# Expert layer: second-key picks from dot 176, four groups a dot; VectorE makes the first keys' one-hots of all tokens; loads asked for when a place comes free

## What is computed

```python
q = (xn @ wq).reshape(B, L, 8, 256)
s1, s2 = q[..., :128] @ k1, q[..., 128:] @ k2      # scores of first and second keys
v1, i1 = top_k(s1, 16); v2, i2 = top_k(s2, 16)
top_s, pos = top_k(v1[..., :, None] + v2[..., None, :], 16)
idx = i1 * 128 + i2 at pos                          # expert = first key, second key
h = gelu(U[idx] . x)                                # 128 dots a token
w = softmax(top_s) * h
y = sum over the 128 experts of w * V[idx]
```

## Time and profile before

| | us |
|---|---|
| median of 3 runs | 3921.55 (3917.01 to 3927.07) |
| profiled execution, its own time | 3927.68 |
| its span in the trace | 3926.0 |
| TensorE busy | 3713.0 (95%) |
| VectorE busy | 1619.5 (41%) |
| GpSimd busy | 876.8 (22%) |
| ScalarE busy | 662.3 (17%) |
| TensorE's granted clock, mean | 0.977 of full |

### The profile page before, as it was taken

One profiled execution on the slowest core, in us unless ns is written; L12 is line 12 of the kernel. 1 busy time (PEld: TensorE's weight loads), 2 busy tenths in 40 slices (PEclk: granted clock), 3 DMA queues, 4 the chain that ended last, 5 costly groups with the idle time before them and its releaser, 6 DMA issues. The chain is left out here.

```text
span 3926.0 us, 43545 instructions
## 1 busy us (share of the span) xinstructions
PE 3713.0 (95%) x17442; PEld 3168.7 (81%) x17442; DVE 1619.5 (41%) x3495; ACT 662.3 (17%) x1544; POOL 876.8 (22%) x781
## 2 busy tenths in 40 slices
PE   8999999999999999992787999998999999999999
PEld 6878887888888888882676777776888899999888
DVE  5883011100000798656546544445234544444200
ACT  0002102100011122220386100000221122222100
POOL 0001000000000344447743455554100111112000
PEclk9999989999999999996999999999999999999999
DMA  5434432344554799998774699998333322222342
GB/s 213 141 129 149 139 108 81 134 150 150 195 198 167 258 375 381 390 384 286 239 230 146 252 337 331 342 333 318 125 118 125 122 92 92 88 85 68 139 155 100
DMA packets 158692, 771.97 MB, mean 197 GB/s; under 512 B 19444, under 2 KB 21388, under 8 KB 122780
## 3 DMA queue, kind: packets, MB, share of 16 engines
q1 hardware_dynamic: 100248, 514.33, 37.1%
q0 software_dynamic: 57344, 251.69, 17.8%
q10 hardware_dynamic: 900, 3.17, 0.2%
HBM read 760.57 MB, written 8.54 MB: 196 GB/s over the span
## 5 line engine op out<-in xcount | busy, mean ns | idle before, releaser
L355 PE MATMUL PS<-mem,ring 128*128 128x256 f32 (+1 forms) x4608 | 1035.8, 388 | 3.0 <-DMA ring<-in_first_tiles 3.0
L355 PEld LDWEIGHTS PS<-mem,ring 128*128 128x128 f32 x4608 | 883.3, 192 | 154.1 <-issue 5.3
L1995 PE MATMUL PS<-mem,ring 128*128 128x256 f32 x2816 | 640.1, 383 | 9.9 <-DVE ring L2393 9.9
L1995 PEld LDWEIGHTS PS<-mem,ring 128*128 128x128 f32 x2816 | 530.9, 192 | 79.4 <-issue 11.0
L1093 POOL DMA_INDIRECT mem<-in_peer_ug,idx x256 | 309.2, 1208 | 1201.1 <-DVE idx L1606 911.6
L1662 DVE CUSTOM_DVE_ANT_0 mem<-mem 128x1152 f32<-128x1152 f32 x256 | 348.5, 1362 | 146.4 <-DMA mem<-in_peer_ug,idx 144.9
L1206 PE MATMUL PS<-mem 128*128 128x256 f32 x1792 | 386.9, 379 | 0.0
L1741 DVE SCALAR_TENSOR_TENSOR mem<-mem 128x768 f32<-128x768 f32 x256 | 261.4, 1021 | 291.7 <-DMA mem<-in_peer_vg,idx 286.6
L1206 PEld LDWEIGHTS PS<-mem 128*128 128x128 f32 x1792 | 340.4, 190 | 46.2
L1118 POOL DMA_INDIRECT mem<-in_peer_vg,idx x256 | 279.3, 1091 | 291.0 <-DVE mem L1741 228.6
L1283 PE MATMUL PS<-mem,ring 128*128 128x512 f32 (+1 forms) x768 | 297.3, 523 | 1.5 <-DMA mem<-in_peer_vd 1.5
(11 more groups left out here) (354 smaller groups left out, 3232.4 us busy)
## 6 DMA issues: line engine op xcount, KB each, us to landing
ring<-in_first_tiles SPq DMA_DIRECT2D x144, 1024.0 KB, 4.8
ring<-in_dn_tiles SPq DMA_DIRECT2D x88, 1024.0 KB, 4.9
mem<-in_peer_vd SPq DMA_DIRECT2D x128, 640.0 KB, 6.7
mem<-in_peer_ud SPq DMA_DIRECT2D x128, 448.0 KB
ring<-in_out_panels SPq DMA_DIRECT2D x16, 2048.0 KB, 8.6
ring<-in_w_out SPq DMA_DIRECT2D x8, 2048.0 KB, 9.3
ring<-in_peer_wq SPq DMA_DIRECT2D x8, 2048.0 KB, 9.5
mem<-second_keys SPq DMA_DIRECT2D x64, 256.0 KB
```

The costliest lines, as they stand in the source:

```text
L355: last = nc.tensor.matmul(PS[:, 4 + n % 4, 0:T if wide else TX], wslot[:, slot_of[n], k, :], x, start=(k == 0), stop=(k == KT - 1))
L1995: ins = nc.tensor.matmul(bank_of(n), wts[:, n % WS, k, :], hT[:, k, :], start=(k == 0), stop=(k == KT - 1))
```

## The change

Picks begin at dot 176 (`PICK0 = 11 * PTOP`) and go four groups a dot for eight dots, then one a dot for two, and from dot 186 (`PAIR0`) VectorE's queue goes pair by pair in TensorE's order: `first` of two tokens, and the 0 or 1 pick groups that TensorE has behind these tokens' scatters, 60 pairs over 68 dots. So VectorE makes `first` of all 256 tokens, 120 of them between the dots. ScalarE makes `second` of tokens 0 to 127; of the second half's, VectorE makes one in eight, ScalarE three, GpSimd four. SyncE's loop asks for the keys of group g + 4 and for chunk n + 2 where it asked for g + 2 and n before; the first two chunks are asked for ahead of the loop.

```diff
-        NPG, FIRST_PICK, SPREAD = P // 4, 13, 28
+        NPG, PICK0, PER, AHEAD = P // 4, 11 * PTOP, 4, 2
+        PAIR0, NPAIR = PICK0 + NPG // PER + AHEAD, 60
+        SPREAD = HN * PTOP - 2 - PAIR0
+        def pairs_at(at):
+            s = at - PAIR0
+            return range(s * NPAIR // SPREAD, (s + 1) * NPAIR // SPREAD) if 0 <= s < SPREAD else range(0)
...
+        def second_groups(s):
+            return AHEAD + (NPG - AHEAD) * s // NPAIR
+        def pair_groups(s):
+            return range(NPG + second_groups(s), NPG + second_groups(s + 1))
+        def early_groups(at):
+            s = at - PICK0
+            if 0 <= s < NPG // PER:
+                return range(s * PER, (s + 1) * PER)
+            return range(NPG + s - NPG // PER, NPG + s - NPG // PER + 1) if NPG // PER <= s < NPG // PER + AHEAD else range(0)
...
+                    for n in range(2):
+                        memory_weights(n)
                     for g in range(MT * NPG):
-                        if PG <= g + 2 < MT * NPG:
-                            second_keys(g + 2)
+                        if g + PG < MT * NPG:
+                            second_keys(g + PG)
                         for n in range(chunks_with(g - 1), chunks_with(g)):
-                            if n >= 2:
-                                sp.wait_ge(kvc_done, n - 1)
...
+                            if n + 2 < NKV * KT // 2:
+                                memory_weights(n + 2)
...
-                                for x in range(HOT0 + 3, MT * P, 4):
+                                for x in range(P + 1, MT * P, 2):
...
                     for g in range(NPG, NPG + AHEAD):
                         turn(g)
                     weight_transpose(0)
-                    for n in range(HOT0):
-                        scatter(n)
-                        if n % 2:
-                            for g in range(NPG + second_groups(n // 2), NPG + second_groups(n // 2 + 1)):
-                                turn(g)
+                    for s in range(NPAIR):
+                        scatter(2 * s)
+                        scatter(2 * s + 1)
+                        for g in pair_groups(s):
+                            turn(g)
...
+                    for n in range(P):
+                        if n == 2 * NPAIR:
+                            for p in range(panel, NKV):
+                                kv_evict(p)
+                            panel = NKV
+                            gelu(1)
+                        second_hot(n)
+                        if n % 4 == 3 and n > 3:
+                            w_evict(n // 4 - 1)
...
+                    weights_turned(1)
+                    w_evict(P // 4 - 1)
+                    for n in range(P, MT * P, 8):
+                        second_hot(n + 2)
+                        if n > P:
+                            w_evict(n // 4 - 1)
+                        second_hot(n + 4)
+                        second_hot(n + 6)
+                        w_evict(n // 4)
...
+                        if n >= OS:
                             dve.wait_ge(oh_used, n - OS + 1)
+                        if m and n % 8 == 0:
+                            nc.vector.tensor_scalar(second[:, n % OS, :], iota[:, :], turnk[:, m, 1, t:t + 1], None, ALU.is_equal)
...
+                            if at == PAIR0:
+                                dve.wait_ge(tw_out, 1)
+                            for g in early_groups(at):
+                                pick_sums(g)
+                            for s in pairs_at(at):
+                                one_hots(2 * s)
+                                one_hots(2 * s + 1)
+                                for g in pair_groups(s):
+                                    pick_sums(g)
```

More of the change, by code:

```diff
@@ L941, in build @@
         beside = {n: (2 * n + 2, 2 * n + 3) for n in range(HN // 2 - 1)}
-        NPG, FIRST_PICK, SPREAD = P // 4, 13, 28
-        def pick_groups(at):
[L947 to L953, removed]
+        NPG, PICK0, PER, AHEAD = P // 4, 11 * PTOP, 4, 2
[13 more added lines that the diff above has]
+            return range(NPG + s - NPG // PER, NPG + s - NPG // PER + 1) if NPG // PER <= s < NPG // PER + AHEAD else range(0)
+        def pick_groups(at):
+            return itertools.chain(early_groups(at), *(pair_groups(s) for s in pairs_at(at)))
         assert [g for at in range(HN * PTOP) for g in pick_groups(at)] == list(range(MT * NPG))
-        HOT0, TURN1, AHEAD = 80, 84, 2
-        def second_groups(s):
-            return AHEAD + (NPG - AHEAD) * 2 * s // HOT0
         def chunks_with(g):
@@ L1298, in _ @@
                     weight_transpose(0)
-                    for n in range(HOT0):
-                        scatter(n)
-                        if n % 2:
-                            for g in range(NPG + second_groups(n // 2), NPG + second_groups(n // 2 + 1)):
-                                turn(g)
+                    for s in range(NPAIR):
[3 more added lines that the diff above has]
+                            turn(g)
                     picked_transpose(1)
-                    for n in range(HOT0, MT * P):
-                        if n == TURN1:
+                    for n in range(2 * NPAIR, MT * P):
+                        if n == P - 4:
                             weight_transpose(1)
@@ L1418, in hot, with second_hot @@
                         return nc.scalar.activation(x, x, ACT.Relu, bias=1.0, scale=-1.0)
[L1420 to L1427, removed]
+                    def second_hot(n):
+                        if n >= OS:
+                            act.wait_ge(oh_used, n - OS + 1)
+                        hot(second[:, n % OS, :], 1, n).then_inc(hot_act, 1)
                     for h in range(PH):
@@ L1467, in _ @@
                     weights_turned(0)
[L1468 to L1473, removed]
+                    for n in range(P):
[7 more added lines that the diff above has]
+                            w_evict(n // 4 - 1)
+                        if n % 2 and panel < NKV and chunks_with(NPG + second_groups(n // 2) - 1) >= KT // 2 * (panel + 1):
                             kv_evict(panel)
                             panel += 1
[L1476 to L1486, removed]
+                    weights_turned(1)
[7 more added lines that the diff above has]
+                        w_evict(n // 4)
                     w_evict(MT * P // 4 - 1)
@@ L1664, in _ @@
                                                            accum_out=dots[:, m, h * PTOP + j:h * PTOP + j + 1]).then_inc(u_used, 1)
[L1665 removed]
+                            if at == PICK0:
                                 softmax_gates()
                                 dve.wait_ge(it_out, 1)
[L1668 removed]
+                            if at == PAIR0 - AHEAD:
                                 whole_dots(0)
[L1670 removed]
+                            if at == PAIR0 - AHEAD + 1:
                                 weights(0)
[L1672 removed]
+                            if at == PAIR0:
+                                dve.wait_ge(tw_out, 1)
+                            for g in early_groups(at):
                                 pick_sums(g)
+                            for s in pairs_at(at):
[3 more added lines that the diff above has]
+                                    pick_sums(g)
                             for _ in range(len(runs) + (j % 4 == 3)):
@@ L1678, in _ @@
                     whole_dots(1)
-                    dve.wait_ge(tw_out, 1)
-                    for n in range(HOT0, MT * P):
-                        if n == TURN1:
+                    for n in range(2 * NPAIR, MT * P):
+                        if n == P - 4:
                             weights(1)
```

35 lines of the change are left out of this document (14 added, 21 removed).

## The result

The changed kernel takes 3878.49 us (median of 4, 3874.79 to 3882.87) against 3923.23 us for the kernel before beside it, a ratio of 0.9888 (95% interval 0.987 to 0.9905): 44.7 us less. Run again later with six executions it had 3881.90 against 3915.49 us, 0.992 (0.9901 to 0.9939), 33.6 us less. So the gain is 34 to 45 us by the medians; 50 was forecast, and 3872 for the time. The changed kernel differs by 3 us between the two comparisons, the kernel before by 8.

A forecast was written before the change was run, and what follows sets the result against it. Engine work and waits between the dense products bound it: start to 1779, picks 69, first scatter 11, pairs 210, tail 65 end at 2134 instead of 2184; 50 us off the median 3921.55 gives 3872, range 3831 to 3900.

The forecast's parts named there:

- What bounds: Between the dense products: only the 417 us from 1767 to 2184 can shrink; dense V behind keeps its 547 us.
- Start: After the dense product: the 62.86 us TensorE gap becomes about 10, ended by the load of the memory's rows.
- First picks: Groups 2 to 31: GpSimd the largest at 2.03 a group, 2.3 taken, 69 us, done at 1848.
- the allowance from 2.05 to 2.3 a group: Groups 2 to 31: 2.3 taken over the bound 2.05, as four places of keys and gathers have to turn round.
- To the first scatter: From the first half's sums to the first scatter: 11 us taken against 16 before, reaching 1859.
- Pairs: Sixty token pairs among the dots: 3.5 us each instead of 4.28, 210 us, dots ending at 2069.
- The coupling: In the pairs: VectorE's sums wait 1.5 us for TensorE's scatters and picks, once per two pairs, 0.75 a pair.
- the DMA floor: In the pairs: 996 KB a pair at 310 to 358 GB/s, 2.8 to 3.2 us, a second limit near VectorE's 3.3.
- my argument that no stretch with keys and gathers mixed had its DMA engines above 0.84: Against pairs at 3.05 us, in a rival of 3831 us (chance 0.15): that pace needs DMA shares of 0.9 to 1.
- Tail: Behind the dots: 136 tokens left instead of 176, ScalarE's 3.1 us per eight, 65 us against 81, ending at 2134.
- The rival of GpSimd held off in the tail: VectorE holds each GpSimd one-hot 0.28 longer, eight tokens take 3.95, 14 us, 3886; within the weaker cases' 0.16.
- Loads asked for earlier: First picks: the 17.6 us wait for memory weights should go, as chunks are asked for about 7 us ahead.

The follow-up runs named there:

- the sums later: Changed kernel, but VectorE takes a group's sums one pair later, behind the next pair's one-hots: 3862.59 us, ratio 0.9862 to the kernel before.
- the old asking: Changed kernel with SyncE's loop put back, keys of group g + 2 and chunk n in loop g: 3887.94 us, ratio 0.9934 to the kernel before.
- the sums later and less loaded: Changed kernel with group sums one pair later and keys and memory weights loaded by half, partly old numbers: 3850.02 us, ratio 0.9837 to the kernel before.
- less loaded: Changed kernel with keys and memory weights loaded by half, same instructions, partly old numbers: 3878.76 us, ratio 0.9902 to the kernel before.
- the first keys' one-hots on ScalarE: Changed kernel, but ScalarE makes both one-hots of tokens 0 to 119 again: 3893.22 us, ratio 0.9942 to the kernel before.

## Why the prediction was right, step by step

*What bounds.* Right: the gain lies between the dense products, and what is saved there arrives whole. From the last scatter to the end of the span it is 1738 to 1743 us in every trace.

*Start.* Right: 10.8 us from the last dense product to the first chunk (10 taken), ended by a load. The profile names the load of memory weights for this wait, and not the memory's rows that I had named. The weights stand right behind the rows in SyncE's queue, and the trace does not tell which of the two held TensorE longer. The two rows show it, TensorE's timeline:

```profile
1762.47 2.02 PE L1242 MATMUL PS<-ring,mem 128*128 128x128 f32 x16 [0.35 <-ACT mem L1466]
1772.07 3.75 PE L1260 MATMUL PS<-mem 128*128 128x256 f32 x8 [7.58 <-DMA mem<-in_mem_w_kv]
```

*First picks.* The size was right: 71.3 us from the first chunk to group 32, 71 in my sum, 2.3 a group. The limit was not: I had GpSimd's work as the largest, and the second stretch of the table of busy time above has TensorE at 60.4 and GpSimd at 56.4 of 69 us. GpSimd waits 18.8 us there for second keys, and TensorE 8.5 us for GpSimd:

```profile
POOL mem L1116 <- DMA mem<-second_keys: 18.8, 9, 8.0
...
PE PS L1242 <- POOL mem L1116: 8.5, 11, 2.1
```

Halving the loads took 7 us off, which is 2.1 a group. So the allowance from 2.05 to 2.3 a group, made for places that have to turn round, stands for waits for loads.

*To the first scatter.* 14.8 us, 11 taken. TensorE was busy 8.2 us of it, near the 7 of my sum, and waited for weights only 1.6; so the rest of the chain (gelu, turned weights and one-hots) is longer than I had it.

*Pairs.* 213.5 us from the first scatter to the end of the last dot (2071.7) for 210. The coupling is shown by taking it away; the DMA floor, which I set beside it as a second limit "so near", is refuted as a limit of this kernel, and waits for loads come up only when the coupling is gone. The size 3.5 is in part luck: I had added 0.2 a pair for the DMA engines, while VectorE's own work was sized at 2.55 and measured 162/60 = 2.7, and its waits at 0.75 and measured 51.8/60 = 0.86. These errors cancelled. Nor is the wait a term that can be taken out of such a sum: without most of it a pair was shorter by 0.27. And my argument that no stretch with keys and gathers mixed had its DMA engines above 0.84 misread, where 1916 to 1932 has 0.87; with the sums later the pairs ran at 0.87.

*Tail.* 64 us from the end of the last dot for 65; eight tokens take 3.14 us, 3.1 taken, as VectorE's timeline shows:

```profile
2086.31 0.29 DVE L1658 TENSOR_SCALAR mem<-iota,mem 128x128 f32<-128x128 f32 x1 [0.47 <-PE PS L1285]
2086.51 2.42 DVE L1659 TENSOR_SCALAR mem<-iota,mem 128x128 f32<-128x128 f32 x8
2089.45 0.29 DVE L1658 TENSOR_SCALAR mem<-iota,mem 128x128 f32<-128x128 f32 x1 [0.51 <-PE PS L1285]
```

The rival of GpSimd held off in the tail did not come true: its one-hots took 0.60 to 0.72 us there, 0.66 in the median, for 0.60 before, far from the 0.28 more that it needed.

```profile
L1128 POOL TENSOR_SCALAR mem<-iota,mem x64: 596/660/722, 2078.8 to 2134.1; 128x128 f32<-128x128 f32 x64
```

*Loads asked for earlier.* Mis-sized: 15 us in my sum, 6 to 10 measured in the changed kernel, 0 in the kernel before, where GpSimd stood behind. The gain existed only together with the new order. In the changed kernel's variant with the old asking TensorE's clock in the pairs was 0.88 too, so a part of these us can be the clock. The section of the Trainium skill that the prediction names here (DMA: Bandwidth & Descriptors, Anatomy of one DMA) gives its fit for DMAs that GpSimd issues; these loads are SyncE's, so the 5.2 us are no test of it. That asking earlier brought nothing in the kernel before is no support for it either: the waits were there, 17.6 us, and went, but GpSimd's took their place.

*The parts.* Taken out one at a time from 374: the new asking 10, the one-hots 13, the early start 13 us of section; the tail is 17 shorter than before. They sum to 53, 43 were gained: they are no independent terms.

*The total.* 50 was forecast. In the same reading, from the last dense product on, the sum has 367 us (2134 - 1767) and the trace 374.2: 7 us too few, about 4 of them on the way to the first scatter and 3.5 in the pairs. That leaves 43. From there to the 34 to 45 of the medians there is a base that was read in one of the longest executions of the kernel before; that this makes up the rest is likely but was not tested with a second trace. That the last dot and the last scatter stand at 2070.3 and 2135.5, as good as the forecast 2069 and 2134, is luck: this trace reached the last dense product 5.4 us earlier.

## What to carry to other kernels

When two engines work in one order, look at what stands in an in-order queue right behind the instruction that lets the other one start: moving the consumer one step later took away 16 us here, with no instruction added. A wait seen in a trace is worth what the next limit leaves of it (40 us of waits, 16 of time; the load waits were worth nothing alone), so test a part in the kernel in which it is to stand, not only by itself. And compare stretches between events of the trace, but take the size of the gain from the medians.

## What the runs showed of the hardware that was not expected

TensorE's granted clock was low where it had stood idle: 0.54 over the hole of 63 us, and 0.82 over the 12 us at the same place after. Among the pairs the traces differ too: 0.93 in the changed kernel, 0.89 with less loaded, 0.88 with the first keys' one-hots on ScalarE, 0.99 with the sums later and less loaded, and the same work kept TensorE busy 167, 173 and 145 us there. No run holds the clock fixed, so each difference of a few us between pairs can be in part the clock's. Halving key and weight loads lowered the DMA share among the pairs from 0.84 to 0.72 and the rate from 274 to 227 GB/s and gained no time, so a share of 0.84 was no sign of a limit.

A dot and one of GpSimd's 128x512 one-hots at the same time cost GpSimd time. Of its 64 in the changed kernel 44 took 1.55 to 1.61 us and 20 took 1.86 to 2.79, each of the 20 beside dots for 0.4 us or more. The dots mostly kept their 1.35 us; three of them took 1.52 to 1.76, one of these here:

```profile
1913.51 1.76 DVE L1672 CUSTOM_DVE_ANT_0 mem<-mem 128x1152 f32<-128x1152 f32 x1
1913.98 2.72 POOL L1116 TENSOR_SCALAR mem<-mem 128x512 f32<-128x512 f32 x1
```

That the dots are the cause is read from the overlap in the trace; no run takes one of the two away.
